# Norms by halves of the tokens, and weight slabs split by two engines

## What is computed

```python
h = rms_norm(x, mix_norm_g);  p = h @ w_in              # mixer 1: gated MLP, convolution, gated delta rule
x = x + mix @ w_out
h = rms_norm(x, ffn_norm_g)
x = x + (silu(h @ w_gate) * (h @ w_up)) @ w_down        # ffn0
x = rms_norm(x, final_norm_g)                           # end of block 1
# block 2: 16 meta tokens are put in front, 1040 tokens
x = x + 0.5 * swiglu(rmsnorm(x, ffn1_norm), w1, w3, w2) # ffn1
p = rmsnorm(x, mix_norm) @ w_in_2                       # mixer 2: window attention and a state space model, glu
x = x + gated @ w_out_2
x = x + 0.5 * swiglu(rmsnorm(x, ffn2_norm), w1, w3, w2) # ffn2
out = rmsnorm(x, final_norm)[meta tokens cut off]
```

## Time and profile before

| | |
|---|---|
| time, median of 3 runs | 4127.27 (4126.79 to 4128.02) |
| the profiled execution | 4125.97, its span 4124.2 |
| TensorE busy | 3722.5 (90%) |
| VectorE busy | 1851.9 (45%) |
| Pool busy | 1531.2 (37%) |
| ScalarE busy | 598.5 (15%) |
| mean granted clock of TensorE | 0.952 of full speed |
| chain that ended last | TensorE 73%, VectorE 20%, issue 3%, ScalarE 2% |

### The profile page before, as it was taken

The page is one execution under the profiler, slowest core; times in us unless marked ns, Lnnn a source line. Parts: engine busy times, 40 slices in busy tenths (PEclk is TensorE's granted clock), DMA queues, the critical chain, the costliest instruction groups (busy, mean ns, idle before and its releaser), DMA issues.

```text
span 4124.2 us, 52854 instructions
## 1 busy us (share of the span) xinstructions
PE 3722.5 (90%) x20662; PEld 3162.4 (77%) x20662; DVE 1851.9 (45%) x2660; ACT 598.5 (15%) x1204; POOL 1531.2 (37%) x718
## 2 busy tenths in 40 slices
PE   5977788879999998899999979998888879999997
PEld 2756578668888886899999978887666668888886
DVE  3299566452121217422222286683777762121216
ACT  3132322110000000200000012113443010000000
POOL 3333200354444443444444453322113454444443
PEclk8989899789999999999999989999999989999998
DMA  2110000111111111111111112101002311111111
GB/s 93 36 31 26 21 1 1 61 31 46 51 45 48 45 49 43 30 42 51 41 51 46 40 47 106 55 27 44 29 24 84 117 32 46 51 41 51 46 49 63
DMA packets 56807, 189.86 MB, mean 46 GB/s; under 512 B 6112, under 2 KB 6240, under 8 KB 56032
## 3 DMA queue, kind: packets, MB, share of 16 engines
q1 hardware_dynamic: 45792, 147.20, 11.8%
q10 hardware_dynamic: 10880, 40.78, 2.6%
HBM read 170.05 MB, written 16.84 MB: 45 GB/s over the span
## 4 chain that ended last, share of the span: by engine, by line
PE 73%; DVE 20%; issue 3%; ACT 2%; POOL 1%; DMA 1%; DVEq 0%; POOLq 0%; ACTq 0%
PE acc L560 21%; PE acc L561 21%; PE acc L562 21%; DVE cv_acc L1123 2%; DVE tmp L528 2%; ACT sc L1566 1%; PE acc L846 1%; DVE ssq L648 1%; PE acc L857 1%; DVE st L1790 1%; DVE cvo L1106 1%; PE acc L856 1%; DVE sq L647 1%; PE acc L497 1%; DVE rs L518 1%
## 5 line engine op out<-in xcount | busy, mean ns | idle before, releaser
L449 POOL TENSOR_TENSOR w_hi<-w_raw,consts 128x1024 fp32r<-128x1024 f32 (+3 forms) x316 | 683.8, 2164 | 2127.8 <-PE acc L562 1861.4
L560 PE MATMUL acc<-h_hi,w_hi 128*128 128x512 f32 (+2 forms) x3552 | 1321.3, 372 | 102.4 <-issue 60.0
L561 PE MATMUL acc<-h_lo,w_hi 128*128 128x512 f32 (+2 forms) x3552 | 1320.0, 372 | 0.0
L562 PE MATMUL acc<-h_hi,w_lo 128*128 128x512 f32 (+2 forms) x3552 | 1312.6, 370 | 0.0
L560 PEld LDWEIGHTS acc<-h_hi,w_hi 128*128 128x128 f32 x3552 | 674.3, 190 | 218.5 <-issue 112.5
L561 PEld LDWEIGHTS acc<-h_lo,w_hi 128*128 128x128 f32 x3552 | 672.8, 189 | 103.4 <-issue 2.7
L562 PEld LDWEIGHTS acc<-h_hi,w_lo 128*128 128x128 f32 x3552 | 673.5, 190 | 99.2
L451 POOL TENSOR_TENSOR w_lo<-w_raw,w_hi 128x1024 fp32r<-128x1024 f32 (+3 forms) x316 | 726.0, 2297 | 24.8
L614 DVE TENSOR_TENSOR ff_hi<-tmp,acc 128x512 f32 (+3 forms) x154 | 94.5, 613 | 1119.6 <-PE acc L562 1106.0
L562 PE MATMUL acc<-ff_hi,w_lo 128*128 128x512 f32 (+2 forms) x1232 | 446.8, 363 | 0.0
L560 PE MATMUL acc<-ff_hi,w_hi 128*128 128x512 f32 (+2 forms) x1232 | 446.1, 362 | 0.0
(11 more groups left out here) (301 smaller groups left out, 3647.5 us busy)
## 6 DMA issues: line engine op xcount, KB each, us to landing
w_raw<-in_ffn_w_dram SPq DMA_DIRECT2D x88, 512.0 KB, 3.5
w_raw<-in_w_in_dram SPq DMA_DIRECT2D x56, 512.0 KB, 3.6
w_raw<-in_ffn_w_dram SPq DMA_DIRECT2D x32, 384.0 KB, 3.0
w_raw<-in_w_gate_dram SPq DMA_DIRECT2D x22, 512.0 KB, 3.5
w_raw<-in_w_up_dram SPq DMA_DIRECT2D x22, 512.0 KB, 3.5
w_raw<-in_ffn_w_dram SPq DMA_DIRECT2D x32, 320.0 KB, 2.9
w_raw<-in_w_out_dram SPq DMA_DIRECT2D x16, 512.0 KB, 3.5
gates_kept<-gstage ACTq DMA_DIRECT2D x32, 256.0 KB, 2.0
```

The lines of the kernel that those rows point to most:

```text
L449: own.link(pool.tensor_tensor(hi.rearrange(blocks, n=P), raw.rearrange(blocks, n=P), ones.unsqueeze(1).broadcast_to([P, seg.kt, P]), ALU.m ...
L560: pe.matmul(bank, wh, rh, start=(k == 0), stop=False)
L561: pe.matmul(bank, wh, rl, start=False, stop=False)
L562: ins = pe.matmul(bank, wl, rh, start=False, stop=(k == seg.kt - 1))
```

## The change

- **Segments.** `out1`, `out2` and the last down segment of each ffn become two segments, `...a` and `...b` (`halves`): all eight slabs over the first half of the columns, then all eight again over the second. The first two pairs of each ffn's up0 and the two pairs of `at_u` are cut the same way (`early_a`, `early_b`). Each of these slabs is loaded and split twice. `CH2` is now 264, 264 and 512 columns; its first half is the first two chunks.
- **Norms.** `act_turn` and `dve_turn` work a turn by halves: ScalarE squares each residual tile (`square`), VectorE adds it; the mean of half 0 is taken behind the first slab of segment b, and its reciprocal, scaled tiles (`t`) and low parts (`l`) are put between the residuals of segment b in the order of `TURN_DVE`. Half 1 follows (`TURN_REST`) while TensorE works on the early slabs of half 0; its mean stands behind the first of these. All low parts are VectorE's now.
- **Final norm of block 1.** Folded into ffn1's norm with `fold_g` and `fold_root`; the meta columns are normed during ffn0 (`dve_meta`), and the final norm itself is written to `x` at the end of ffn1's first up segment (`act_fin`, `dve_fin`, `pe_fin`).
- **The end.** Normed into `x` by halves, with four output transfers for each.
- **Slab splits.** ScalarE writes the high part (`w_high`, a copy) at fixed places of its own program (`w_after`, `w_pair`, `w_segment`), each time that of the slab two further on; Pool waits for it and writes the low part in four quarter pieces (`LOW_PIECES`).

```diff
-CH2 = [(0, 352), (352, 344), (696, 344)]
+CH2 = [(0, 264), (264, 264), (528, 512)]
+EARLY = 2
+LOW_PIECES = 4
...
+    def halves(name, pairs, kt, chunks, src):
+        add(name + "a", pairs, kt, chunks[:-1], src)
+        add(name + "b", pairs, kt, chunks[-1:], src, lambda i, j, c: 3 * j + len(chunks) - 1)
...
+        def w_high(act, seg, i, j):
+            width = seg.kt * P
+            act.wait_ge(raw_full[j], (i + seg.n0 // 2 + 1) * 16)
+            if seg.n0 or not isinstance(i, int) or i:
+                act.wait_ge(acc_full[j], i * len(seg.chunks) + seg.q0)
+            act.copy(w_hi[:, j, 0:width], w_raw[:, j, 0:width]).then_inc(sem("w_high"), 1)
...
-                    own.link(pool.tensor_tensor(hi.rearrange(blocks, n=P), raw.rearrange(blocks, n=P),
-                                                ones.unsqueeze(1).broadcast_to([P, seg.kt, P]), ALU.mult))
-                    pool.tensor_tensor(lo, raw, hi.bitcast(F32), ALU.subtract).then_inc(split_done, 1)
+                    pool.wait_ge(sem("w_high"), i * 2 + (seg.n0 + j + 1))
+                    step = width // LOW_PIECES
+                    for a in range(0, width, step):
+                        ins = pool.tensor_tensor(w_lo[:, j, a:a + step], w_raw[:, j, a:a + step], w_hi[:, j, a:a + step].bitcast(F32),
+                                                 ALU.subtract)
+                    ins.then_inc(split_done, 1)
...
+        def pe_early(pe, name, segs):
+            h, u = (h_hi, h_lo), 2 * TURNS.index(name)
+            pe_ready(pe, name, 0)
+            pe_slab(pe, segs[0], 0, 0, h)
+            pe_mean(pe, name, 1)
+            pe_slab(pe, segs[0], 0, 1, h)
+            pe.wait_ge(sem("sd_done"), parts_until(u + 2))
+            for j in range(2):
+                pe_slab(pe, segs[0], 1, j, h)
+            pe_ready(pe, name, 1)
+            for i in range(EARLY):
+                for j in range(2):
+                    pe_slab(pe, segs[1], i, j, h)
...
+            for s in range(KD):
+                square(0, s)
+                w_after(act, segs[0], s // 2, s % 2)
+            for s in range(KD):
+                square(1, s)
+                w_after(act, segs[1], s // 2, s % 2)
+                if s == 0:
+                    root(0)
+                for k in TURN_HI[s]:
+                    if not final:
+                        high(0, k)
+                    elif k % 2:
+                        store(0, k)
+            if when_read:
+                when_read()
+            root(1)
+            for k in range(KD):
+                if not final:
+                    high(1, k)
+                    if k in (2, 5):
+                        w_after(act, SEG[NEXT_SEG[segs[1].name]], 0, k // 3)
+                elif k % 2:
+                    store(1, k)
...
+        TURN_HI = [(), (), (0, 1, 2), (3, 4), (5, 6), (7,), (), ()]
+        TURN_DVE = [(), (("r", 0),), (("t", 0), ("t", 1), ("t", 2)), (("l", 0), ("t", 3), ("l", 1), ("t", 4)),
+                    (("l", 2), ("t", 5), ("l", 3), ("t", 6)), (("l", 4), ("t", 7), ("l", 5)), (("l", 6), ("l", 7)), ()]
+        TURN_REST = [("r", 0), ("t", 0), ("t", 1), ("t", 2), ("l", 0), ("t", 3), ("l", 1), ("t", 4), ("l", 2), ("t", 5),
+                     ("l", 3), ("t", 6), ("l", 4), ("t", 7), ("l", 5), ("l", 6), ("l", 7)]
...
+            for s in range(KD):
+                residual(1, s)
+                if s > 1:
+                    add(1, s - 1)
+                for what, k in TURN_DVE[s]:
+                    piece(0, what, k)
...
+            if i == SEG["ffn1_up0"].pairs - 1:
+                for half in range(2):
+                    cols = fin_columns(half)
+                    dve.wait_ge(sem("fin_sd"), half + 1)
+                    own.link(dve.reciprocal(rs[:, cols], rs[:, cols]))
+                    for k in range(KD):
+                        own.mark(dve.scalar_tensor_tensor(x[:, k, cols], x[:, k, cols], param("final_g")[:, k:k + 1], rs[:, cols],
+                                                          ALU.mult, ALU.mult))
```

More of the change, by code:

```diff
@@ L161, in slab_plan @@
[L161 to L172, removed]
@@ L173, in slab_plan @@
-    if "ffn2" in parts:
-        ffn("ffn2", t["ffn2_w1_2"], t["ffn2_w3_2"], t["ffn2_w2_2"], CH1)
-    return segs
+            if part == 0:
+                first, second = early_banks(chunks)
+                add(f"{name}_early_a", EARLY, KD, chunks[:-1], pair(wg, wu), first)
+                add(f"{name}_early_b", EARLY, KD, chunks[-1:], pair(wg, wu), second)
+            skip = 0 if part else EARLY
+            add(f"{name}_up{part}", nf - skip, KD, chunks, pair(wg, wu, f + skip))
+            if part < len(FQ) - 1:
+                add(f"{name}_down{part}", KD // 2, nf, chunks, run(wd[part], 0))
+            else:
+                halves(f"{name}_down{part}", KD // 2, nf, chunks, run(wd[part], 0))
@@ new lines, in ffn @@
+            f += nf
+    add("gm", 2, KD, CH1, run(t["w_in"], 0))
+    add("cv", 2, KD, CH1, run(t["w_in"], 4))
+    add("dn_kv", 4, KD, CH1, run(t["w_in"], 12))
+    add("dn_q", 2, KD, CH1, run(t["w_in"], 8))
+    add("dn_g", 2, KD, CH1, run(t["w_in"], 20))
+    halves("out1", 4, KD, CH1, run(t["w_out"], 0))
+    ffn("ffn0", t["w_gate"], t["w_up"], t["w_down"], CH1)
+    ffn("ffn1", t["ffn1_w1_2"], t["ffn1_w3_2"], t["ffn1_w2_2"], CH2)
+    first, second = early_banks(CH2)
+    add("at_ua", 2, KD, CH2[:-1], run(t["w_in_2"], 12), first)
@@ new lines, in slab_plan @@
+    add("at_ub", 2, KD, CH2[-1:], run(t["w_in_2"], 12), second)
+    add("at_g", GATES_A, KD, CH1, run(t["w_in_2"], 16))
+    add("at_q", 4, KD, CH1, run(t["w_in_2"], 0))
+    add("at_kv", 2, KD, CH2, run(t["w_in_2"], 8))
+    add("at_h", 8 - GATES_A, KD, CH1, run(t["w_in_2"], 16 + 2 * GATES_A))
+    add("glu", 8, KD // 2, CH1, pair(t["ssm_glu_b_2"], t["ssm_glu_a_2"]))
+    halves("out2", 4, KD, CH1, run(t["w_out_2"], 0))
+    ffn("ffn2", t["ffn2_w1_2"], t["ffn2_w3_2"], t["ffn2_w2_2"], CH1)
+    return segs
@@ L455, in _ @@
+                if name not in ("gm", "out1a"):
+                    with pool.Fori(0, seg.pairs) as i:
                         for j in range(2):
@@ L582, in pe_ffn @@
+                down = SEG[f"{name}_down{part}"]
                 for c in range(len(chunks)):
```

614 lines of the change are left out of this document (393 added, 221 removed).

## The result

The changed kernel takes 4017.71 us (median of 4, 4017.56 to 4018.13) against 4127.42 of the kernel before on the same chip: ratio 0.9734, 95% interval 0.9718 to 0.9751. I had forecast 4088 with a range of 4048 to 4122; the gain is 110 us and not 39. First, its page: the span and the busy time of each engine.

A forecast was written before the change was run, and what follows sets the result against it. TensorE was taken to bound the ffn bodies, so gains lay in the turns and in mixer 1, where VectorE is the bound and Pool stretches it. Terms summed to -39 us, 4126.0 to 4087, forecast 4088, range 4048 to 4122.

The forecast's parts named there:

- The state space scan ... against ScalarE's eight more copies in the attention: Scan and attention together: scan freed from Pool's stretching, set against ScalarE's added copies, -3 us, between -8 and +8.
- What a turn cost before: TensorE's gaps between segments plus 2.0 us of low clock each: 27.6, 49.7, 32.3, 27.6 and 26.2 us, 163 in all.
- What a turn costs after: The five turns in the changed kernel, forecast at 18.5, 35, 33.5, 25.4 and 30.3 us.
- The early slabs: First slabs behind a turn: TensorE idles 7.6 us, 1.8 at lower clock, second half's weights late; +12.5 with the mean.
- The halves with kt = 5: Last down segments: weights and norm pieces late, +6 first half, +10 second; at the kernel's end +6 and +7.5.
- The moved final norm: Behind ffn1's up0: VectorE needs 22.5 us while two down slabs last 17; 4.7 idle and 1.8 low clock.
- The first rival: The halves hide what was priced as lost: 52 us of half-slab terms go, 4036 us; chance 0.17.
- Mixer 1, start, glu: Mixer 1 -17 from shorter Pool holds on VectorE; start +3 and +5 from ScalarE's copies; behind the glu -6.
- The alternative of 14.5 us by a full lock: Mixer 1: every quarter locks for its whole 0.74, Pool keeps 3.0 of 4.7, winning 14.5 and not 17.
- the zero for the widths: Ffn bodies: new CH2 has the same columns and as many matmuls, 264-column ones 0.122 us apart, so no change.
- Two rivals: Slower: ScalarE's queue holds weights back in the mixers, 4146, chance 0.05; weight-load floor at 264 columns, 4153, 0.04.
- The second rival: Pool's four quarters follow each other before VectorE gets in; mixer 1 gains nothing, second halves lose 8: 4113; chance 0.14.

The follow-up runs named there:

- old_supply: The changed kernel with Pool writing both the high and the low part of each slab whole, ScalarE none, halves kept: 4137.26 us, ratio 1.0024.

## Why the prediction was wrong

The direction held, and so did the mechanisms of mixer 1 and of the turns; the one of the attention was missing, and the size was off: 107.9 us of span against 39. The mixers gave 54 where the sum had 18, the turns 54 where it had 21. The 69 missing us have four sources. No single one explains the miss: with the attention right the sum would have been -63.

- **"The state space scan ... against ScalarE's eight more copies in the attention: -3, an estimate by the size of the mixer 1 term"** is the step that failed: -26.9, 24 us of the 69. No row of the attention was read for it. The term carried the loss of a stream over to the state space scan (-2.3) and gave the attention nothing but ScalarE's copies. In mixer 1 VectorE is busy without a pause, but many of its operations don't meet Pool, and it lost 41 us to 90 us of Pool's pieces. In the attention TensorE and ScalarE wait for VectorE, so a hold costs its full length, even for an operation of two columns: some 29 us were lost to 33 us of pieces. The 3.8 us gaps of TensorE there were to be seen in the trace before.
- **What a turn cost before** was read from its gap plus 2 us of low clock, 163 in all. Measured from stage to stage, less the pace of the bodies, it was 179 (31.4, 54.3, 36.6, 30.5, 26.2). In turn B, for one, the body behind the gap took 143.6 instead of 136.9 us: beside the low clock, TensorE waited 2.3 us in front of the last chunk (1689.90) and 1.5 for a slab's weights (1699.15). 16 us.
- **What a turn costs after** came to 125.5 (16.4, 28.7, 32.4, 23.0, 25.0) against 142.7 forecast. The early slabs, forecast at 12.5, cost 10.4 in turn A, 11.6 in turn B and 10.0 in turn D, their mean included. The halves with kt = 5, forecast at 6 + 10 and 6 + 7.5, cost 4.3 + 8.0 and 3.9 + 4.7. The moved final norm cost 4.7 and not 6.5 (22.5 less 17 would even have given 5.5 of idle time, not the 4.7 that I wrote). Together 17 us. The first rival wanted all 52 us of the halves' terms to go; some 7 went. The stepping through was sound and a little too dear.
- **Mixer 1, start, glu**: -23.3 for -17, +4.5 for +8, -8.7 for -6. Together 12 us, right in kind. In mixer 1 what VectorE lost to Pool fell to 39% (15.8 of 40.7) and not to 55%. The alternative of 14.5 us by a full lock stood beside 17, from which 1 had been taken off already; the like figure is 13.5, further still from the measured 23.3.

The prediction's price of a piece held (0.74 for 256 columns, measured 0.73), as did the zero for the widths in the bodies. Two rivals died: ScalarE's queue shows no loss in the mixers but 4.5 us at the start, and there is no floor at 264 columns. (The records of the weight loads themselves last 188 ns in the median, before and after, and overlap one another, so the load of 107 ns can't be read from them.) The second rival, that quarters don't help VectorE, was wrong for the attention (344.1 whole, 334.2 in quarters). In mixer 1 quarters won 7 us beside a whole high part on Pool (664.5 to 657.4) and nothing clear once that had left (642.6 to 641.2); the larger share there, 16 to 22 us, came from the high part leaving Pool.

What I had not asked at all is whether the halves pay without the supply. They don't. My sum stepped the halves through with the new supply only, so it could not show that they would lose with the old one.

## What to carry to other kernels

Before a term is called small, look in the trace at how the loop waits: the same hold of Pool on VectorE cost under half of its length in a stage where VectorE also had work that Pool doesn't touch, and nearly its full length in a loop where engines take turns. Splitting norms so that they run beside matmuls paid here only when the engine that does them got through beside the weight splits and the weights were still in time. Try the parts of such a change in a square, not one after the other. And choose the size of a piece by place: in this kernel whole where the weights are late, small where another engine streams or waits its turn.

## What the runs showed of the hardware

- Which operations of VectorE wait for Pool. In the fences above a tensor_tensor and a scalar_tensor_tensor on 2 columns, both inputs in SBUF, waited 1.3 and 1.7 us, and the fp32 tensor_scalar of 272 columns 2.0; a copy out of PSUM (0.28) ran at full speed beside Pool's pieces. In the kernel before, the residual's add of 512 columns, with one input in PSUM, took 0.69 us in all 71 cases that began inside a piece of Pool, as in the 89 others, and the reciprocal of 512 columns 3.35 in 3 and in 7; the split `ff_lo<-tmp,ff_hi` of 512 columns, with both inputs in SBUF, took 1.44 on average inside and 0.69 outside. The Trainium skill (SBUF — State Buffer, "SBUF: two separate sides") names as the contenders VectorE's operations in a 2-port mode or "with two SBUF inputs"; the trace agrees for the operations named here, though it doesn't show in which mode the tensor_scalar ran. The prediction had used that rule without this list.
- Where both engines have work queued they alternate piece by piece: 3 tiles of VectorE took 8.52 us between Pool's pieces of 2.4 to 2.7 in old_supply. So a long piece on one side sets the pace of short ones on the other.
- A piece of Pool's fp32 subtraction has a fixed price of 0.19 us (2.366 us for 1024 columns, 0.730 for 256, 0.462 for 128). Eighths in place of quarters, 0.9 us more a slab, made the turns 40 us longer.
